# Attention in a two-layer hybrid trunk: exponentials taken from query-major scores, scaled, then turned on TensorE

## What is computed

```python
def one_block(qblk):                       # A; context tokens do it with B's sink too
    s = jnp.einsum('bqkgd,blkd->bkgql', qblk, k).astype(jnp.float32)
    p = jax.nn.softmax(s, axis=-1)
    return jnp.einsum('bkgql,blkd->bqkgd', p.astype(v.dtype), v)
# B: band of three key tiles and cached context, plus the sink
valid = (jnp.abs(q_pos - k_pos) <= WINDOW) & (k_pos >= 0) & (k_pos < N)
p = jax.nn.softmax(jnp.concatenate([s_band, s_ctx, s_sink], axis=-1), axis=-1)
o = p_band @ vband + p_ctx @ v_ctx         # the sink has no value
```

## Time and profile before

| | us |
|---|---|
| median of 3 runs | 1519.32 (1518.76 to 1519.97) |
| the profiled execution, its own time | 1520.94 |
| its span | 1519.1 |
| PE busy | 1445.8 |
| DVE, POOL, ACT busy | 796.1, 771.7, 587.9 |
| share of PE in the chain that ended last | 87% |
| mean granted TensorE clock | 0.986 of full speed |

### The profile page before, as it was taken

One profiled execution on the slowest core, in us unless ns is written; L12 is line 12 of the kernel. 1 busy time (PEld: TensorE's weight loads), 2 busy tenths in 40 slices (PEclk: granted clock), 3 DMA queues, 4 the chain that ended last, 5 costly groups with the idle time before them and its releaser, 6 DMA issues.

```text
span 1519.1 us, 21747 instructions
## 1 busy us (share of the span) xinstructions
PE 1445.8 (95%) x8776; PEld 1306.1 (86%) x8776; DVE 796.1 (52%) x1164; ACT 587.9 (39%) x934; POOL 771.7 (51%) x554
## 2 busy tenths in 40 slices
PE   5999999999998999999979999998999999999996
PEld 3898889889887888999868988897988879999985
DVE  4675676452677520312784747764436775022157
ACT  4334564233764311213243346542357632222140
POOL 2454676323676443344674557753246755443443
PEclk9999999999999999999999999999999999999998
DMA  8412000212000443444320220012110013215221
GB/s 336 126 56 74 29 28 21 90 47 83 28 29 28 132 156 122 141 159 139 124 98 28 88 70 15 29 56 73 56 57 28 29 53 113 76 62 198 96 99 70
DMA packets 36756, 126.90 MB, mean 84 GB/s; under 512 B 5040, under 2 KB 5680, under 8 KB 36656
## 3 DMA queue, kind: packets, MB, share of 16 engines
q1 hardware_dynamic: 29952, 108.54, 21.3%
q10 hardware_dynamic: 6704, 16.97, 3.1%
HBM read 119.73 MB, written 5.77 MB: 83 GB/s over the span
## 4 chain that ended last, share of the span: by engine, by line
PE 87%; DVE 5%; POOL 3%; issue 2%; ACT 2%; DVEq 0%; POOLq 0%; ACTq 0%
PE ps L910 46%; PE ps L858 7%; PE ps L860 7%; PE ps L859 7%; PE ps L1045 3%; PE ps L1043 2%; PE ps L1095 2%; PE ps L1072 2%; PE ps L1071 2%; PE ps L1092 2%; PE ps L1093 2%; PE ps L927 1%; POOL w_lo L1764 1%; DVE o_inv L1633 1%; PE ps L1102 1%
## 5 line engine op out<-in xcount | busy, mean ns | idle before, releaser
L1764 POOL TENSOR_TENSOR w_lo<-raw,w_hi 128x1024 fp32r<-128x1024 f32 x148 | 360.1, 2440 | 359.0 <-ACT w_hi L1138 358.7
L910 PE MATMUL ps<-h_hi,w_hi 128*128 128x320 f32 x1280 | 299.3, 315 | 18.4 <-DVE g_c L1645 8.0
L910 PE MATMUL ps<-h_hi,w_lo 128*128 128x320 f32 x1280 | 292.6, 310 | 0.0
L910 PE MATMUL ps<-h_lo,w_hi 128*128 128x320 f32 x1280 | 292.6, 310 | 0.0
L1792 POOL TENSOR_TENSOR p_lo<-p_f,p_hi 128x512 fp32r<-128x512 f32 x164 | 211.9, 1296 | 139.0 <-ACT p_hi L1298 138.2
L910 PEld LDWEIGHTS ps<-h_hi,w_hi 128*128 128x128 f32 x1280 | 217.3, 189 | 39.3 <-DVE g_c L1645 9.8
L910 PEld LDWEIGHTS ps<-h_lo,w_hi 128*128 128x128 f32 x1280 | 215.9, 189 | 2.2
L910 PEld LDWEIGHTS ps<-h_hi,w_lo 128*128 128x128 f32 x1280 | 215.6, 189 | 2.2
L1138 ACT ACTIVATE w_hi<-raw 128x1024 fp32r<-128x1024 f32 x148 | 152.8, 1051 | 92.1 <-DMA raw<-in_weights 53.7
L1589 DVE TENSOR_REDUCE top<-ps 128x1 f32<-128x512 f32 (+1 forms) x128 | 83.7, 658 | 144.7 <-PE ps L1050 105.0
L1660 DVE TENSOR_TENSOR gy<-ps,sg 128x640 f32<-128x640 f32 x32 | 26.4, 824 | 241.2 <-PE ps L910 241.1
(11 more groups left out here) (180 smaller groups left out, 2599.2 us busy)
## 6 DMA issues: line engine op xcount, KB each, us to landing
raw<-in_weights SPq DMA_DIRECT2D x190, 512.0 KB, 3.4
raw_more<-in_weights SPq DMA_DIRECT2D x10, 512.0 KB, 10.6
x<-in_x_sample ACTq DMA_DIRECT2D x6, 512.0 KB, 8.0
x_mid<-x ACTq DMA_DIRECT2D x5, 512.0 KB, 2.6
x<-x_mid ACTq DMA_DIRECT2D x5, 512.0 KB, 6.5
y_sample<-x SPq DMA_DIRECT2D x3, 512.0 KB, 2.6
pack<-in_pack ACTq DMA_DIRECT2D x2, 528.0 KB, 4.8
x<-in_x_sample SPq DMA_DIRECT2D x2, 512.0 KB, 4.9
```

The lines of the kernel that those rows point to most:

```text
L910: last = pe.matmul(ps[:, s + half, 0:HALF], w[:, u % RING, cols], acts[:, k, half * HALF:(half + 1) * HALF], start=k == 0 and part == 0, s ...
L1764: did(pool.tensor_tensor(w_lo[:, n % RING, :], raw_tile(r), w_hi[:, n % RING, :], ALU.subtract), w_ready)
```

## The change

`ST`, `row`, `es`, `ones` and the sink slot go. Instead:

- `ex`: ACT takes the exponentials straight from the query-major scores of `S`, with minus the maximum (`neg`, one column for each head, from DVE) as bias, and sums along the keys by the accumulator output (`sums`). P lies in `p_f` with queries on the partitions. In A the cached unit comes first and is copied to `cached`, its part is exponentiated head by head. In B, exp(sink - maximum) is added to the sum.
- `iv`: once for a group, DVE takes the reciprocals of the sums (four columns) and scales P in place, four operations of up to 640 columns.
- `T`: PE turns P by slots, four transposes into a bank; ACT writes `p_hi`; `pl`: DVE writes the low half out of PSUM.
- `PV`, two steps behind: two passes. The stationary operand is the high half of the values in 64 columns and the low half in the other 64 (`vv`), so rows 0 to 63 of the output hold high values times P and rows 64 to 127 low values times P.
- `O`: ACT copies the low rows to `o_low`, DVE adds the two halves.
- The scores of group g may begin when the group two before has been turned (two buffers of P). The first gate stage of the filler stands between the first scores: seven stages in A, nine in B. No weight split stands between a group's last score and its `iv` (`held`).

```diff
-    early = {n: [] for n in range(-1, len(steps))}
-    start = -1
+    scores = {n: [] for n in range(-1, len(steps))}
+    exps = {n: [] for n in range(-1, len(steps))}
+    inverses = {n: [] for n in range(-1, len(steps))}
     for g in range(count):
         units = [("S", l, br, g, u) for u in range(len(score_units(br, g)))]
-        end = max(first[g] - score_ahead, -1)
+        holder = p_place(g)[2]
+        start = -1 if holder < 0 else first[holder + 1] - 1
+        end = max(first[g] - ahead, start)
         for i, e in enumerate(units):
-            early[start + (end - start) * (i + 1) // len(units)].append(e)
-        early[max(first[g] - row_ahead, -1)].append(("row", l, br, g))
-        if br == "b":
-            early[max(first[g] - row_ahead, -1)].append(("es", l, br, g))
-        start = end
-    for n in early:
-        early[n].sort(key=lambda e: (e[0] == "S", e[3]) if n >= 0 else (e[3], e[0] != "S"))
+            at = start + (end - start + 1) * i // len(units)
+            assert at >= -1 and (holder < 0 or at >= first[holder + 1] - 1)
+            scores[at].append(e)
+            exps[at].append(("ex", *e[1:]))
+        inverses[end if end < 0 else end + 1].append(("iv", l, br, g))
...
-        out.append(("ST", l, br, g, i))
-        out.extend(early[n])
+        out.append(("T", l, br, g, i))
+        out.extend(scores[n])
+        out.append(("pl", l, br, g, i))
         tick()
         if n >= lag:
             product(n - lag)
         fill()
+        out.extend(inverses[n])
+        out.extend(exps[n])
...
-                        key = slice(KEY_PLACE[slot_key] * P, (KEY_PLACE[slot_key] + 1) * P)
-                        heads, tokens = group_heads(g)
-                        pe.matmul(ps[:, s, :], k_hi[:, kv, key], q_t[:, heads, tokens], start=True, stop=False)
-                        last = pe.matmul(ps[:, s, :], k_lo[0:TOP_ROW + GRP, kv, key], q_m[0:TOP_ROW + GRP, n % 3, :],
-                                         start=False, stop=mask is None)
-                        if mask is not None:
-                            block = 2 if mask == "before" else 0
-                            last = pe.matmul(ps[:, s, :], ident_r[:, :], mask_r[:, block:block + 1, :].to_broadcast([P, GRP, P]),
-                                             start=False, stop=True)
+                        n = NO[("iv",) + e[1:4]]
+                        pe.wait_ge(over_sum, n + 1)
+                        for h in range(GRP):
+                            last = pe.transpose(ps[:, s, h * P:(h + 1) * P], p_part(br, g)[:, h, i * P:(i + 1) * P], ident)
                         did(last, filled[s])
...
-                        if slot_key == SINK:
-                            high = one_row[:, kv:kv + 2, :].rearrange("p s d -> p (s d)")
-                            pe.matmul(ps[:, b, :], high, p_hi[:, n % 3, :], start=False, stop=False)
-                        else:
-                            high, low = v_blocks(slot_key, kv)
-                            pe.matmul(ps[:, b, :], high, p_hi[:, n % 3, :], start=i == 0, stop=False)
-                            pe.matmul(ps[:, b, :], low, p_hi[:, n % 3, :], start=False, stop=False)
-                        pe.wait_ge(p_lo_made, n + 1)
-                        last = pe.matmul(ps[:, b, :], high, p_lo[:, n % 3, :], start=False, stop=ends)
+                        values = vv[:, key, kv, :, :].rearrange("p s d -> p (s d)")
+                        pe.matmul(ps[:, b, :], values, p_hi[:, n % 3, :], start=i == 0, stop=False)
+                        wait_drained(pe, ("T",) + e[1:])
+                        last = pe.matmul(ps[:, b, :], values, p_low(br, n), start=False, stop=ends)
                         did(last, filled[b] if ends else pv_done)
...
+                    elif kind == "ex":
                         _, l, br, g, i = e
+                        scores, unit, c = ("S",) + e[1:], score_units(br, g)[i], NO[("iv",) + e[1:4]]
+                        s = wait_filled(act, scores)
+                        if l and (br, g, i) == ("a", 0, 0):
+                            for t in range(T):
+                                act.wait_ge(x_kept[t], 16)
+                        act.wait_ge(neg_made, NEG_NO[scores])
+                        if unit == "cache":
+                            did(act.activation(cached[:, g % 2, :], ps[:, s, :], ACT.Copy), drained[s])
+                            continue
+                        if br == "b" and unit in ("heads", GRP - 1):
+                            act.wait_ge(es_d_made, ES_NO[scores])
+                            act.activation(sums[:, c % 3, 1, :], es_d[:, c % 3, :], ACT.Exp)
+                        for h in range(GRP) if unit == "heads" else (unit,):
+                            p, bias = p_part(br, g)[:, h, :], neg[:, c % 3, h:h + 1]
+                            if br == "a" and unit != "heads":
+                                wait_drained(act, ("S", l, br, g, 0))
+                                act.activation(p[:, LAT * P:], cached[:, g % 2, h * P:(h + 1) * P], ACT.Exp, bias=bias,
+                                               accum_out=sums[:, c % 3, 1, h:h + 1])
+                                p = p[:, 0:LAT * P]
+                            n = p.shape[-1]
+                            src = ps[:, s, h * P:(h + 1) * P] if unit == "heads" else ps[:, s, 0:n]
+                            last = act.activation(p, src, ACT.Exp, bias=bias, accum_out=sums[:, c % 3, 0, h:h + 1])
+                        did(last, drained[s])
+                    elif kind == "T":
+                        s = wait_filled(act, e)
                         n = NO[e]
                         if n >= 3:
-                            act.wait_ge(p_lo_made, n - 2)
                             product = ("PV",) + STEPS[n - 3][1:]
                             if product in PV_NO:
                                 act.wait_ge(pv_done, PV_NO[product])
                             else:
                                 wait_filled(act, ("O",) + product[1:4])
...
+                        did(act.activation(p_hi[:, n % 3, :], ps[:, s, :], ACT.Copy), p_hi_made)
...
+                            h, n = unit, len(group_slots(br, g)) - (br == "a")
+                            after(did(dve.tensor_reduce(best[:, h:h + 1], ps[:, s, 0:n * P], axis=AX.X, op=ALU.max)))
+                            other = others[:, h:h + 1] if br == "a" else sinks[:, h:h + 1]
+                            did(dve.tensor_scalar(neg[:, c, h:h + 1], best[:, h:h + 1], other, -1.0, ALU.max, ALU.mult), neg_made)
+                        if br == "b" and unit in ("heads", GRP - 1):
+                            dve.wait_ge(neg_made, NEG_NO[e])
+                            did(dve.tensor_tensor(es_d[:, c, :], sinks, neg[:, c, :], ALU.add), es_d_made)
+                    elif kind == "iv":
                         _, l, br, g = e
+                        c = NO[e] % 3
+                        wait_drained(dve, ("S", l, br, g, len(score_units(br, g)) - 1))
+                        total = sums[:, c, 0, :]
+                        if br == "b" or GROUPS[g][1]:
+                            after(did(dve.tensor_tensor(total, total, sums[:, c, 1, :], ALU.add)))
+                        after(did(dve.reciprocal(inv[:, c, :], total)))
+                        for h in range(GRP):
+                            part = p_part(br, g)[:, h, :]
+                            last = dve.tensor_scalar(part, part, inv[:, c, h:h + 1], None, ALU.mult)
+                        did(last, over_sum)
+                    elif kind == "pl":
+                        _, l, br, g, i = e
+                        n, s = NO[e], PLACE[("T",) + e[1:]][0]
+                        dve.wait_ge(p_hi_made, n + 1)
+                        did(dve.tensor_tensor(p_low(br, n), ps[:, s, :], p_hi[:, n % 3, :], ALU.subtract), drained[s])
+                    elif kind == "O":
+                        _, l, br, g = e
+                        b = wait_filled(dve, e)
                         n = NO[e]
+                        dve.wait_ge(o_low_made, n + 1)
                         for odd in range(2):
+                            last = dve.tensor_tensor(og_sum(n)[head_rows(odd), :, :], by_head(ps[0:HD, b, :])[:, odd:GRP:2, :],
+                                                     by_head(o_low[HD:P, n % 2, :])[:, odd:GRP:2, :], ALU.add)
+                            did(last, drained[b] if odd else None)
...
-    for j in range(2, KT_D):
+    for j in range(1, KT_D):
         filler.extend(chunks(("z", l, 0, j), 8))
         filler[-1] = (filler[-1], ("z", l, 0, j))
-    out.extend(flat(attention(l, "a", filler[:-5], filler[-5:], 3, 2, 4)))
+    out.extend(flat(attention(l, "a", filler[:8], filler[8:-5], filler[-5:], 2, 3)))
...
-    out.extend(flat(attention(l, "b", filler[:-3], filler[-3:], 3, 2, 4)))
+    out.extend(flat(attention(l, "b", filler[:6], filler[6:-3], filler[-3:], 2, 3)))
...
```

(48 more changed lines are left out.)

230 lines of the change are left out of this document (73 added, 157 removed).

## The result

The changed kernel takes 1607.18 us (median of 4 runs, 1604.84 to 1609.28) beside 1519.04 (1516.89 to 1519.97) for the kernel before: ratio 1.058, 95% interval [1.056, 1.060]. It is 88 us slower where 27 us faster was forecast, and lies above the whole range. The profiled execution has a span of 1605.5 us.

What follows compares the result with a forecast made beforehand. TensorE sets the a stages; after the change, a chain through three engines. Two a stages +6.5 us each, two b -18.8 each, memsets -2: -26.6; 1520.9 - 27 = 1494, 1.6 lower for the median: 1492. Range 1448 to 1524.

Steps and rivals of the forecast that it cites:

- Scores stay.: Attention stages, TensorE: the score passes keep their old cost, 22.7 us in an a stage and 19 in a b.
- The order keeps splits out between last score and scaling: Attention groups: no weight split runs between a group's last score and its scaling; argued against a 1562 us outcome.
- the port rival: GpSimd's splits hold up VectorE's scaling or negation, 2.42 us lost per group: 1562 us; chance 0.17, shared with slow clock.
- the chain laid out by hand: Attention groups, three engines in order: 14.1 us a group in a; a stages about 131 us, b about 118.5.
- PE's floors: Attention stages: TensorE's work alone after the change takes 110 us in a and 109.5 in b.
- The transposes: TensorE, each step with keys: four transposes take 0.36 us and lengthen the next matmul by 0.08, 0.44 in all.
- DVE over 85% busy in a: Sign that the forecast is right: VectorE busy over 85% of the a stages.
- Accumulating exponential: ScalarE: summing along the keys adds 0.08 us to each exponential (bounds 0 and 0.19), 1.15 us per a head.
- scaling: VectorE, once a group: four in-place scalings of 640 columns at a pitch of about 0.55 us, 2.2 us together.
- table load: ScalarE in b: exponentials alternate with Silu gates, ten loads at 1.28 us, 13 us against nine loads before.
- POOL under 40 us: Sign that the forecast is right: GpSimd busy under 40 us in each attention stage.
- The clock rival: Transposes let attention fall to 1.2 GHz for an example tenth of each stage, 48 us more: 1540; chance 0.17, shared.

Runs made afterwards that it cites:

- experiment 6: The changed kernel, its 64-row low-key score pass kept, with weight splits held until the new group's first transposes and scores four steps ahead, not three: 1569.13 us.
- the fastest kernel: The changed kernel with 96-row low-key score passes, splits held until the first transposes, scores three steps ahead in a, four in b: 1499.86 us (0.987).

## Why the prediction was wrong, by its steps

- **"Scores stay."** This step failed. 128 long and 24 short units were kept at the old price though the diff shows L1061 (L1045 before) with `HD` where `TOP_ROW` stood. Worth 55.6 us here, slow clock that comes with it included (experiment 6), and 67.6 in the old kernel, where the clock stays at 1.00. No row of before had a 64-row pass among 128-row ones, so by my own rule the price should have been bounded from both sides; the changed operand shape wasn't seen as an edit.
- **"The order keeps splits out between last score and scaling"**, the argument against the port rival. It failed: `held` ends at `iv` in the list, but ACT and POOL have no part in `iv` and walk past it, so the next split runs at the very time of the scaling. The row for its price stood there, and the rival's mechanism, POOL against the scaling, is what happened: 41.7 to 45.9 us. The rival asked 2.42 us of every group; the 512-column scalings lost 4 x (1095 - 482) = 2.5 us a group on average, the 640-column ones 0.65, the 384-column ones nothing. Over the 32 latent groups that is 0.94 us, so the rival was right in its mechanism and had the number of groups too high; the rest of its 41.7 to 45.9 us is in PE's waits and the slow clock behind them, and wasn't priced apart. It had shared a chance of 0.17 with the clock.
- **The sum of both:** 1607.2 - 55.6 - 41.7 = 1509.9, with 18 us left to 1492. In that kernel a is 125 where I had 131: full groups follow each other 13.2 us apart, not 14.1, so the chain laid out by hand was too serial (that ACT and DVE overlap groups more than laid out is the likely reason, not followed); its terms also add to 128 us, not the 129 written. b is 128.7 where I had 118.5: PE still waits 10.7 us for scalings in the two, before the first group, three of the four with four key tiles and the context groups, and four steps ahead bring 3 us. The rest of b's 10 us a stage stays open. The stages sum to 507.0 for 499; outside them are 1507.6 - 507.0 = 1000.6 us, 7 more than forecast. With three and four steps the stages sum to 499.4, the forecast figure, made of two errors of about 6 us each stage that cancel.
- **PE's floors** of 110 and 109.5 were too low: PE is busy 114.4 to 116.2 at a clock of 0.99 or 1.00. Which passes make up the 5 us wasn't followed. The transposes, 0.36 with 0.08 to 0.09 on the next pass, were right.
- **DVE over 85% busy in a:** wrong; 67% (96.8 of 144.6), and 72 to 74% in the fastest kernel. The term was sound (8 groups x 12.2 = 98 us, 91 to 97 measured), the share wasn't: 12.2 of 14.1 is the share in a full group, not over a stage with a head and a tail.
- **Accumulating exponential, scaling, table load, POOL under 40 us:** right in size (0.67 pitch with the read; 2.2 us for four scalings where no split runs, 1.94 seen; 1.28; 29.5 to 36).
- **The clock rival:** right in part. The granted clock did fall, to 0.87 to 0.95, "under 0.95 in attention" in three stages. In b most of it follows PE's waits (440.9 after the wait at 439.02). In a it doesn't: PE waits 2.0 and 3.4 us there, and most of the low stretches start behind no pause of PE (195.20 above). By experiment 6 these need the 64-row passes together with the change. With the same 576 transposes, 96 rows and few waits the clock is 0.99 to 1.00 in the stages, so the transposes alone don't bring it down. Whether they are the part of the change that does it beside short passes no run tells.

## What to carry to other kernels

Read a diff for operand shapes as carefully as for operations: a pass that shrinks from 96 to 64 rows among passes of 128 cost 0.14 to 0.19 us at each change of height, and more through the clock, where padding it with zero rows cost one fill of 1.55 us a layer. An event that an engine skips doesn't hold that engine: what must not run beside a DVE operation with both operands in SBUF has to stand behind something that waits for it. And a spare step between scores and transposes is to be tried branch by branch: it gave 3 us a stage in b and took 5 in a.

## What the runs showed of the hardware

- TensorE, passes of 64 rows between passes of 128: the pass ahead of one and the pass itself take 0.41 and 0.42 us to the next start for 512 columns (0.32, behind transposes, and 0.23 with 96 rows), 0.25 for 128 columns (0.11); 64 behind 64: 0.11.
- Four scalings of 512 columns in SBUF beside one GpSimd subtraction of 2.53 us: 3.8 to 4.3 us; without it 1.68 to 1.85.
- Waits of PE of 2.35 and 1.00 us close together, and 3.3 us at the 1.2 GHz level (0.50 of full speed) behind them.
- An a stage of the changed kernel with 64-row passes and 2.1 us without a matmul: granted clock 0.86; the kernel before with such passes: 1.00; the changed kernel with 96-row passes and the same order: 0.97.
- An activation with an accumulator output is followed by a read of 0.19 us, of which 0.09 is added to the time to the next activation.
